# Prompt's routing in its own score loop, its product rows in the first half of the sample phase, 64 of its weighted rows on VectorE

## The reference

```python
q = (x @ w_q).reshape(PEER_CHUNK, PEER_HEADS, 2, PK_HALF)
s = jnp.einsum('chpd,hpnd->chpn', q, sub_keys).astype(jnp.float32)
st, it = lax.top_k(s, PEER_TOPK)
cand = (st[:, :, 0, :, None] + st[:, :, 1, None, :]).reshape(PEER_CHUNK, PEER_HEADS, -1)
...
best, pos = lax.top_k(cand, PEER_TOPK)
eidx = jnp.take_along_axis(cidx, pos, axis=-1)
g = jax.nn.softmax(best, axis=-1)
act = jax.nn.gelu(jnp.einsum('chkd,cd->chk', u_tab[eidx], x).astype(jnp.float32))
return jnp.einsum('chk,chkd->cd', (g * act).astype(x.dtype), v_tab[eidx])
```

## Time and profile before

| what | value |
|---|---|
| time, median of 3 runs (lowest, highest) | 2556.26 us (2548.68, 2557.54) |
| the profiled execution's own time | 2556.07 us |
| its span | 2554.3 us |
| PE, matmul | 1918.7 us busy, 75% |
| DVE | 1810.1 us busy, 71% |
| POOL | 1038.4 us busy, 41% |
| ACT | 478.6 us busy, 19% |
| DMA queues | 753.45 MB, 295 GB/s over the span |
| chain that ended last, by engine | DVE 28%, PE 26%, DMA 23%, POOL 12%, issue 7% |

### The profile page before, as it was taken

One profiled execution on the slowest core, in us unless ns is written; L12 is line 12 of the kernel. 1 busy time (PEld: TensorE's weight loads), 2 busy tenths in 40 slices (PEclk: granted clock), 3 DMA queues, 4 the chain that ended last, 5 costly groups with the idle time before them and its releaser, 6 DMA issues.

```text
span 2554.3 us, 20828 instructions
## 1 busy us (share of the span) xinstructions
PE 1918.7 (75%) x6333; PEld 1128.8 (44%) x6333; DVE 1810.1 (71%) x3850; ACT 478.6 (19%) x1213; POOL 1038.4 (41%) x1028
## 2 busy tenths in 40 slices
PE   6779789999988969983557777769999999000085
PEld 2568664444466437541113333456666666000032
DVE  1341306868786576698989888788777876999955
ACT  0361114540033001111013223460000000000011
POOL 0000000001523460226767777534444446777674
PEclk9899899999999979995769999879999999555599
DMA  8656672124844892548999999869999999999997
GB/s 287 216 171 219 214 233 72 34 89 140 310 145 158 295 326 86 199 142 319 409 409 382 410 410 410 322 205 412 416 407 412 411 411 411 410 409 409 374 398 308
DMA packets 296873, 753.45 MB, mean 295 GB/s; under 512 B 21502, under 2 KB 141102, under 8 KB 296244
## 3 DMA queue, kind: packets, MB, share of 16 engines
q0 software_dynamic: 147456, 536.94, 54.4%
q1 hardware_dynamic: 149308, 215.20, 24.0%
HBM read 740.72 MB, written 11.33 MB: 294 GB/s over the span
## 4 chain that ended last, share of the span: by engine, by line
DVE 28%; PE 26%; DMA 23%; POOL 12%; issue 7%; ACT 3%; SPq 0%; ACTq 0%; DVEq 0%; POOLq 0%
PE bank L755 8%; DMA attn<-in_peer_u_dram,eidx 6%; PE pair L755 6%; POOL big L1992 4%; DMA ring_more<-in_peer_u_dram,eidx 4%; DVE attn L1467 4%; PE bank L929 3%; POOL attn L1992 3%; DMA big<-in_peer_v_dram,eidx 3%; DMA big<-in_peer_u_dram,eidx 3%; DMA attn<-in_peer_v_dram,eidx 2%; PE bank L977 2%; DMA h_all<-in_peer_u_dram,eidx 2%; POOL ring_more L1992 2%; DVE big L1467 2%
## 5 line engine op out<-in xcount | busy, mean ns | idle before, releaser
L977 PE MATMUL bank<-big,work 128*128 128x512 f32 x376 | 213.4, 702 | 365.2 <-ACT work L1049 263.8
L1992 POOL DMA_INDIRECT h_all<-in_peer_u_dram,eidx x117 | 137.2, 1173 | 787.1 <-DVEq L1606 596.8
L755 PE MATMUL pair<-big 128*128 128x128 f32 (+1 forms) x1280 | 362.4, 441 | 14.0 <-issue 6.2
L1992 POOL DMA_INDIRECT attn<-in_peer_u_dram,eidx x201 | 197.3, 982 | 317.8 <-DVE dots L1467 196.9
L755 PE MATMUL bank<-big 128*128 128x512 f32 (+1 forms) x1056 | 311.0, 456 | 15.6 <-DVEq L1346 4.7
L977 PEld LDWEIGHTS bank<-big,work 128*128 128x128 f32 x376 | 74.1, 213 | 488.4 <-issue 443.4
L1467 DVE CUSTOM_DVE_ANT_0 attn<-attn,pair 128x1024 f32<-128x1024 f32 x201 | 240.6, 1219 | 51.2 <-DMA attn<-in_peer_u_dram,eidx 47.6
L755 PEld LDWEIGHTS pair<-big 128*128 128x128 f32 x1280 | 198.3, 195 | 165.4 <-issue 159.3
L1022 PE MATMUL bank<-h_all,big 128*128 128x512 f32 x608 | 266.9, 595 | 4.6 <-DMA h_all<-in_peer_v_dram 4.6
L755 PEld LDWEIGHTS bank<-big 128*128 128x128 f32 x1056 | 172.6, 205 | 148.7 <-issue 140.9
L1467 DVE CUSTOM_DVE_ANT_0 big<-big,pair 128x1024 f32<-128x1024 f32 x168 | 200.9, 1219 | 35.1 <-DMA big<-in_peer_u_dram,eidx 32.3
(11 more groups left out here) (294 smaller groups left out, 2890.2 us busy)
## 6 DMA issues: line engine op xcount, KB each, us to landing
big<-in_w_in_dram SPq DMA_DIRECT2D x44, 1024.0 KB, 5.4
h_all<-in_peer_v_dram SPq DMA_DIRECT2D x76, 512.0 KB, 6.8
big<-in_w_ada_dram SPq DMA_DIRECT2D x24, 1024.0 KB, 8.5
big<-in_peer_w_q_dram SPq DMA_DIRECT2D x16, 1024.0 KB, 5.8
gf_row<-in_peer_v_dram SPq DMA_DIRECT2D x26, 512.0 KB, 6.7
work<-in_peer_v_dram SPq DMA_DIRECT2D x26, 512.0 KB, 6.8
big<-in_w_rnn_o_dram SPq DMA_DIRECT2D x8, 1024.0 KB, 5.4
big<-in_w_attn_o_dram SPq DMA_DIRECT2D x8, 1024.0 KB, 6.6
```

The source lines that it names most:

```text
L755: last = nc.tensor.matmul(u[:, 0:n], w[:, k, col:col + P], src[:, k, 0:n], start=(k == 0), stop=(k == KD - 1))
L977: last = nc.tensor.matmul(psum[i][:, :], diag[:, (n - 1) % DIAGS, :], ring[r][:, i * 512:(i + 1) * 512], start=(k == first_by_tensor[c]), ...
L1992: g.indirect_dma_start(dst, None, ins["peer_" + table][0], bass.IndirectOffsetOnAxis(ap=eidx[:, c, k:k + 1], axis=0)).then_inc(landed, 16)
```

## The change

It moves the prompt's `topk` and `best_sums` into phase 0's score loop, with `experts` and `ids` of 6 of the 8 heads; 2 heads are left for `serve`. `serve` starts at the end of phase 0, so that its calls in phase 1's recurrent loop take rows (6 in each block; the first two calls take a head each). `gelu_dots(0)` moves ahead of the attention's start. The first 64 weighted rows are then served through the same ring by VectorE into two accumulators (`acc0`, in `gf_row` and `final_row`), and `add_sums(0, acc0)` adds them to x in the mix stage. TensorE keeps 64 weighted rows, 16 in step 0 and 48 in step 1. The calls of `serve` after a `gr` step go from 5 to 7, ahead of `ga` from 4 to 2.

```diff
@@ -264,15 +264,15 @@
...
     steps[0] = [("u", C1, k) for k in range(EARLY)]
-    V0_FIRST, V0_NEXT = 32, 96
+    FRONT, V0_FIRST, V0_NEXT = 64, 16, 48
     for k in range(SLOTS - EARLY):
         n0, n1 = (j * V0_FIRST // (SLOTS - EARLY) for j in (k, k + 1))
-        steps[0] += [("u", C1, EARLY + k)] + [("v", 0, 0 + n) for n in range(n0, n1)]
+        steps[0] += [("u", C1, EARLY + k)] + [("v", 0, FRONT + n) for n in range(n0, n1)]
     steps[1] = []
...
         n0, n1 = (j * V0_NEXT // SLOTS for j in (k, k + 1))
-        steps[1] += [("u", C1 + 1, k)] + [("v", 0, 0 + V0_FIRST + n) for n in range(n0, n1)]
-    assert 0 + V0_FIRST + V0_NEXT == SLOTS
+        steps[1] += [("u", C1 + 1, k)] + [("v", 0, FRONT + V0_FIRST + n) for n in range(n0, n1)]
+    assert FRONT + V0_FIRST + V0_NEXT == SLOTS
     half = SLOTS // 2
@@ -316,7 +316,7 @@
...
     last_by_tensor = {c: k for (table, c, k), b in zip(turns, by) if b == "tensor"}
-    first_by_tensor = {0: 0, C4: ALONE}
+    first_by_tensor = {0: FRONT, C4: ALONE}
     sum_rows = {c: [n for n, (table, c_, k) in enumerate(turns) if table == "v" and c_ == c and by[n] == "vector"]
@@ -430,6 +430,7 @@
...
         assert len(ring0) == RING0
+        acc0 = [gf_row[:, 1, :], final_row[:, :]]
@@ -1151,6 +1152,8 @@
...
                         act.drain().then_inc(rg_ready, 1)
+                if ph:
+                    soft(0)
                 merge("gr", 0)
@@ -1160,9 +1163,9 @@
...
                         run(featT[:, h, 0:N], u[:, 0:N], ACT.Identity).then_inc(bank_free[bank[(ph, "q", h)]], 1)
+                if ph:
+                    gelu_dots(0)
                 end_stage()
-                if ph:
-                    soft(0)
@@ -1202,8 +1205,6 @@
...
                 for t in range(NT[ph] + 1):
-                    if ph and t == 1:
-                        gelu_dots(0)
                     if t < NT[ph]:
@@ -1422,32 +1423,42 @@
...
-            def route0(i):
-                if i < PH:
-                    best_sums(0, i)
-                elif i == PH:
-                    best_diffs(0)
-                elif i <= 2 * PH:
-                    experts(0, i - PH - 1, i - PH)
-                    ids(0, i - PH - 1, i - PH)
-            LEFT0 = 2 * PH + 1
+            gelu0 = [False]
+            HEADS_IN_LOOP = 6
+            LEFT0 = PH - HEADS_IN_LOOP
+            def route0(h):
+                experts(0, h, h + 1)
+                ids(0, h, h + 1)
...
                 for _ in range(n):
-                    if served[0] is None or served[0] == LEFT0 + SLOTS:
+                    if served[0] is None or served[0] == LEFT0 + SLOTS + FRONT:
+                        return
+                    if served[0] == LEFT0 + SLOTS and not gelu0[0]:
                         return
...
                     if s_ < 0:
-                        route0(s_ + LEFT0)
+                        route0(PH + s_)
                         continue
...
                     dve.wait_ge(row0_in[r], 16 * (s_ // RING0 + 1))
-                    V.tensor_tensor_reduce(ring0[r], ring0[r], h2_all[:, 0, :], 1.0, 0.0, ALU.mult, ALU.add,
-                                           dots[:, s_:s_ + 1]).then_inc(slot0_used, 1)
+                    if s_ < SLOTS:
+                        V.tensor_tensor_reduce(ring0[r], ring0[r], h2_all[:, 0, :], 1.0, 0.0, ALU.mult, ALU.add,
+                                               dots[:, s_:s_ + 1]).then_inc(slot0_used, 1)
+                        continue
+                    a_, w_ = acc0[s_ % 2], gw[:, 0, s_ - SLOTS:s_ - SLOTS + 1]
+                    if s_ < SLOTS + 2:
+                        V.tensor_scalar(a_, ring0[r], w_, None, ALU.mult).then_inc(slot0_used, 1)
+                    else:
+                        dve.wait_ge(slot0_used, RING0 + s_ - 1)
+                        V.scalar_tensor_tensor(a_, ring0[r], w_, a_, ALU.mult, ALU.add).then_inc(slot0_used, 1)
@@ -1485,6 +1496,7 @@
...
                     dve.wait_ge(slot0_used, RING0 + SLOTS)
+                    gelu0[0] = True
                     routed(0)
@@ -1704,10 +1716,7 @@
...
                         conv(j + 1)
-                    for hp in (2 * j, 2 * j + 1) if ph else ():
-                        u = (0, "sc", hp)
-                        dve.wait_ge(bank_free[bank[u]], use[u])
-                        topk(-1, hp, scores0[:, hp, :])
+                    serve(2)
                     y = xc[j % 2][:, 0:N]
@@ -1732,9 +1741,7 @@
...
                     dve.drain().then_inc(lru_done, 1)
-                if ph:
-                    dve.drain().then_inc(slot0_used, RING0)
-                    served[0] = 0
+                    serve(1)
                 end_stage()
@@ -1750,7 +1757,7 @@
...
                         dve.drain().then_inc(mix_ready, 1)
-                        serve(5 if a == "gr" else 7)
+                        serve(7 if a == "gr" else 7)
                 serve(6)
@@ -1811,7 +1819,7 @@
...
                 end_stage()
-                serve(4)
+                serve(2)
                 merge("ga", "ao", KD)
@@ -1827,7 +1835,10 @@
...
                     if ph and t == 1:
-                        gelu_dots(0)
+                        serve(FRONT)
+                        dve.wait_ge(slot0_used, RING0 + SLOTS + FRONT)
+                        dve.wait_ge(final_in, 16)
+                        add_sums(0, acc0)
                         dve.drain().then_inc(sums0_done, 1)
@@ -1843,8 +1854,17 @@
...
                     if ph == 0:
+                        u = (0, "sc", hp)
+                        dve.wait_ge(bank_free[bank[u]], use[u])
+                        topk(-1, hp, scores0[:, hp, :])
                         if hp + 1 in ada_after:
                             add_bias(ada_after[hp + 1])
+                        if hp % 2:
+                            best_sums(0, hp // 2)
+                            if hp // 2 < HEADS_IN_LOOP:
+                                route0(hp // 2)
+                        if hp == HP - 1:
+                            best_diffs(0)
                         continue
@@ -1862,6 +1882,9 @@
...
                     dve.drain().then_inc(state_turned, 1)
+                    dve.drain().then_inc(slot0_used, RING0)
+                    served[0] = 0
                 else:
@@ -1992,14 +2015,14 @@
...
-            for n in range(SLOTS):
+            for n in range(SLOTS + FRONT):
                 r = n % RING0
-                if n % TOPK == 0:
+                if n < SLOTS and n % TOPK == 0:
                     pool.wait_ge(head_ready, n // TOPK + 1)
                 pool.wait_ge(slot0_used, n + 1)
-                fetch("u", 0, n, ring0[r], row0_in[r])
-            pool.wait_ge(slot0_used, RING0 + SLOTS)
+                fetch("u" if n < SLOTS else "v", 0, n % SLOTS, ring0[r], row0_in[r])
+            pool.wait_ge(slot0_used, RING0 + SLOTS + FRONT)
             for turn, (table, c, k) in enumerate(turns):
```

## The result

The changed kernel takes 2532.96 us (median of 4 runs, 2531.65 to 2535.14) against 2553.29 us for the kernel before on the same chip (2548.68 to 2557.54): ratio 0.9917, 95% interval 0.9901 to 0.9933. The profiled execution took 2533.43 us with a span of 2531.6, 22.7 us less than the span before. The time lies in the forecast range (2525 to 2580), 20 us under the forecast of 2553 and on the faster side, to which the forecast gave 0.31.

A forecast was written before the change was run, and what follows sets the result against it. The prediction took DMA (403 GB/s) to bound the back's steps 0 and 1, VectorE next, and a hand-ordered TensorE/VectorE chain the front. Front +38.5 and back -42 gave net -3.5, about 2553 us; range 2525 to 2580.

The forecast's parts named there:

- The forecast case: Whole kernel: front +38.5, back -42, net -3.5, about 2553 us; own range 2541 to 2568, chance 0.47.
- the absorbed loop: Rival: the recurrent loop's TensorE path absorbs the rows, only its tail grows, +10 instead of +28, 2535 us; chance 0.20.
- Score loop of prompt: Routing added there holds TensorE 10 to 13 us; the recurrent loop's first body starts at 430 instead of 413.25.
- Recurrent loop, +28: Six product rows replace two `topk` per block, 21.05 us instead of 19.11; the loop ends at 595.5 instead of 567.5.
- the starved ring: Rival: slow refills of the five-slot ring make 46 front rows cost 1.91 us instead of 1.15: +35, 2588; chance 0.14.
- `gr` merge, +3: The merge now holds 62 rows; 117 us to the first rope against 114.7, so +3 us.
- The tail ahead of attention, +21: Last 12 product rows 16 us, `routed` and gelu exchange 3.6, stage signals 1: +21 us (18 to 27).
- Attention, +4.5: 24 weighted rows of 1.285 us replace product rows of 1.15, +3; TensorE starting after a long idle, +1.5.
- `ga`, -18: Fewer rows beside the `ga` merges, the last ending at 924: -18 us, bounded by 24.9.
- The back, -42: Steps 0 and 1: 64 fewer gathers remove VectorE's 46.5 us of waits, less 4.5 for first landings; bounds -47 and -25.
- The rival of the whole DMA time (-83): The back gives all the DMA time of the 64 rows, 83 us instead of 42: 2512 us; chance 0.08.
- gathers that block VectorE: Rival: 46 gathers in the recurrent loop each block two-input VectorE instructions by up to 0.94 us: +43, 2596; chance 0.03.

The follow-up runs named there:

- the run with other banks: Changed kernel with the four late units of the modulation vectors in banks of their own, which VectorE does not hold; 0.9769 of the kernel before, on kind B.
- the run without rows: Changed kernel with no weighted rows in the front, all 128 gathered in the back and summed by TensorE; 1.0064 of the kernel before, on kind B.
- kind A: Chips on which the kernel before takes 2551 to 2553 us; the result was measured on one.
- kind B: Chips on which the kernel before takes 2665 to 2672 us; the changed kernel has 0.976 of it there.
- routing alone: Kernel before with only prompt's routing moved into prompt's score loop, product rows in their old places, no weighted row in the front; 0.9991, on kind B.

## Why the prediction was right, and where its sizes were off

The range and the mechanism held: 64 rows leave a DMA-bound stretch that is then bound by VectorE, against a front that grows by less. The two sums were off by some 10 us each, both to the good side: the front +28.5 instead of +38.5, the back -51.3 instead of -42.

That the time fell into the range is in part luck. The forecast case had a range of its own, 2541 to 2568, and 2533 lies outside it; the wider range had been drawn to hold the rivals too. The nearest single number of the forecast is the 2535 of the absorbed loop, which did not happen. The case's own range doesn't follow from its bounds either: -47 and -25 for the back and 18 to 27 for the tail give 2545 to 2576. By its own steps:

- *Score loop of prompt*: right. TensorE is held 3.0 us at 354.81 and 8.5 us at 374.64, together 11.5 (forecast 10 to 13), body 0 starts at 428.68 (forecast 430), and VectorE's routing is what sets it, shown by the run with other banks. One sum of the forecast is off by 0.7 us: 329.2 + 15.2 + 28.4 + 2 is 374.8, not 375.5.
- *Recurrent loop, +28*: measured +26.5 (the row behind the last gate ends at 594.1; body 7 at 582.46 against 557.83). 20.82 us a block against 21.05, body 6 at 567.61 against 568.5; no landing waits in the loop, so the starved ring didn't happen. The pair in the place of the `topk` is free, shown by removing it. Against the rival of an absorbed loop: it absorbed only that pair.
- *`gr` merge, +3*: the first rope at 709.19 is 27.0 us later than before, so +0.5.
- *The tail ahead of attention, +21*: attention starts 49.4 us later than before, so +22.4.
- *Attention, +4.5*: this term failed. Attention's first instruction and the first `ga` merge are 122.5 us apart, before (719.71 and 842.13) and after. The 1.5 us for a TensorE that starts after a long pause did not come: it had paused 25.7 us instead of 4.4, and the granted clock in attention's first 10 us was 0.90 in both. The other 3 us had priced the row by its duration, 1.285 us; the rows 812.64, 813.84 and 815.04 above start 1.20 us apart, and the run without rows shows that only half of a row is on the path there, so that a difference of 0.05 us a row can't show.
- *`ga`, -18*: measured -20.1: TensorE waits 4.7 us ahead of the mix instead of 24.9. The sum of the front is 26.5 + 0.5 + 22.4 + 0 - 20.1 = 29.3, and the mix gives 0.8 back.
- *The back, -42*: the second term mis-sized. It took 4.5 us off for first landings; 44.6 of the 46.5 us of waits went where 42 had been counted, and 6.7 us more came that had stood at nothing. From first gather to addition VectorE has 1322 instructions in both, busy for 540.6 us before and 533.6 after. Three successive rows of the kernel before show where that comes from:

```profile
1173.98 1.22 DVE L1467 CUSTOM_DVE_ANT_0 big<-big,pair 128x1024 f32<-128x1024 f32 x1
...
1175.13 1.22 DVE L1467 CUSTOM_DVE_ANT_0 big<-big,pair 128x1024 f32<-128x1024 f32 x1
...
1177.15 1.22 DVE L1467 CUSTOM_DVE_ANT_0 big<-big,pair 128x1024 f32<-128x1024 f32 x1 [0.80 <-DMA big<-in_peer_u_dram,eidx]
```

The second row starts 1.15 us after the first, though the first is shown with 1.22: the end of a row overlaps with what follows at once. The third stands behind a wait, so nothing overlaps with the second row's end, and that one costs 1177.15 - 0.80 - 1175.13 = 1.22. Over the whole piece a row costs 1.14 to 1.15 us where the next row or instruction follows at once and 1.23 where it waits. Of the same 264 rows, 76 stand ahead of a wait, however short, in the kernel before and 16 in the changed one: 60 x 0.08 = 4.9 of the 6.7 us. So each wait that goes takes 0.08 us of the row *ahead* of it along. That the upper end of the back was 47 is the bound that failed: its reason, that VectorE's own work stays and the gain ends where its waits end, took VectorE's busy time as fixed.

The rival of the whole DMA time (-83) is refuted on kind A by the run that only leaves out 64 rows. On kind B that run gave -92, but not by that rival's mechanism: the landing waits went (76.9 to 5.1 us) and some idle time without a named releaser with them, and the queue was not full there, as below.

Of gathers that block VectorE: 192 gathers lie beside VectorE's front now, and they still range from 932 to 1991 ns; the 16 of them with no VectorE instruction beside them take at most 940. The 78 product rows below stay at 1214 to 1266 ns. Of all 128 product rows 65 start while a gather runs, and they take at most 1227 ns, as the rows without a gather do. So here too it is GpSimd that is held. The Trainium skill (SBUF — State Buffer, section Who interferes with whom) has whichever starts later block; these rows show one direction only.

```profile
L1452 DVE CUSTOM_DVE_ANT_0 h_all<-h_all x78: 1214/1225/1266, 426.4 to 763.2; 128x1024 f32<-128x1024 f32 x78
```

```profile
L2015 POOL DMA_INDIRECT ring_more<-in_peer_u_dram,eidx x50: 932/961/1991, 412.9 to 753.4; - x50
```

## What to carry to other kernels

A transfer moved out of a DMA-bound stretch is worth its DMA time only until the next engine's waits for it are gone, plus the little that instructions lose by standing ahead of waits (0.08 us each here); price it from the waits, and check it with a run that only leaves the transfers out. The price of work moved to a busy front depends on the place, not on the work: the same VectorE row cost nothing in the loop where ScalarE was awaited, 0.6 to 0.7 us in attention and 1.5 to 1.7 us at a stage's end where everyone waits. The mean slack of a queue can't be spent to its end: going from 64 rows to 48, the mean said free, and it cost 7 us.

## What the runs showed of the hardware that was not expected

The price of a gathered row differed between the two kinds of chips. From first gather to addition, with so many of prompt's weighted rows taken out of the back: on kind A 626.5 us with none (the kernel before), 582.5 with 48, 575.2 with 64: 0.92 us a row at first, then 0.45. On kind B 719.0 with none (routing alone; 735.6 in the run without weighted rows in the front, whose profiled execution is 13 us above its median), 672.2 with 32, 655.4 with 40, 621.4 with 64 (615 to 624 in the five runs with 64), 592.0 with 120: some 1.5 us a row up to 64, then 0.5. The change as it stands is worth 65 us there instead of 20. The price is near what a row takes of the stretch at its mean rate, 524 KB / 334 GB/s = 1.57 us, but the queue is busy only 0.89 of that stretch, where on kind A it was full with 403 GB/s. So the transfers alone don't explain it: the landing waits are worth 72 us for 64 rows (1.1 each), and idle time without a named releaser most of the rest. The window of the run with the routing alone, with the columns of the earlier trace rows:

```profile
1200.00:1700.00 500.00, 298.56 (x706) 133.13 (x705) 364.19 (x872) 93.88 (x302) 305.19 (x311) 0.78 0.89 334
```

From 2000 to 2250 us both kinds move 411 GB/s. Behind the addition kind B is slower once more, 901 to 911 us to the end against 880 to 882, most of it in the last 350 us. What differs in the stretch is seen on VectorE and TensorE: idle time with no named releaser, of which kind A shows at most 0.3 us there. VectorE's waits in that run from 1200 to 1723 us, and two of eight small instructions in a row, each behind 1.2 to 1.3 us in which it waited for nothing that the trace names:

```profile
DVE best L1539 <- remote: 18.6, 2, 10.4
...
DVE work L1531 <- issue: 10.3, 9, 1.3
```

```profile
1218.26 0.18 DVE L1531 TENSOR_TENSOR work<-big 128x16 f32<-128x16 f32 x1 [1.22 <-issue]
1219.67 0.18 DVE L1531 TENSOR_TENSOR work<-big 128x24 f32<-128x24 f32 x1 [1.24 <-issue]
```

At 1320.97 us seven instructions of the same line take 0.69 us together, without such gaps. Late instructions would look like this. The Trainium skill (Runtime: NRT & Kernel Launch, section Instruction fetch mechanics) says that each engine's sequencer fetches its next block over a DMA queue while it works through the current one, and that this is mostly hidden. The trace has the packets of two queues of the kind `instruction`, and from 1183 to 1266 us, around these eight instructions and the wait of 8.3 us behind them, it has none of either; the view of the queues there holds one line:

```profile
q0 software_dynamic: 8068, 29.38, 91.2%
```

So this trace speaks against a late fetch at that place. What else it was, no run here shows, and the cause of kind B stays open.
